# Seven block products in place of eight in ten weight units of a one-core decoder layer

## What is computed

```python
h = rms_norm(x, norm_mix)
proj = h @ w_in                      # (256, 2048) @ (2048, 832 + 3 * 1024)
c_q, c_kv, k_pe, q_sb, k_sb, v_sb = jnp.split(proj, IN_SPLITS, axis=-1)
# latent attention from c_q, c_kv, k_pe; stick-breaking attention from q_sb, k_sb, v_sb
x = x + concat(rms_norm(o_mla), rms_norm(o_sb)) @ w_out
x = x + memory_cross_attention(rms_norm(x), rms_norm(mem), ...)
x = x + hierarchical_moe(rms_norm(x), ...)      # 32 experts, 2 per token
return rms_norm(x, norm_final)
```

## Time and profile before

| | us |
|---|---|
| median of 3 runs | 1351.78 (1351.17 to 1353.06) |
| profiled execution, whole | 1350.58 |
| its span, first to last instruction | 1348.8 |
| PE busy / DVE / ACT / POOL in the span | 992.5 / 576.0 / 303.9 / 40.9 |
| bytes moved by DMA | 486.40 MB, mean 361 GB/s |

### The profile page before, as it was taken

One profiled execution on the slowest core, in us unless ns is written; L12 is line 12 of the kernel. 1 busy time (PEld: TensorE's weight loads), 2 busy tenths in 40 slices (PEclk: granted clock), 3 DMA queues, 4 the chain that ended last, 5 costly groups with the idle time before them and its releaser, 6 DMA issues.

```text
span 1348.8 us, 20643 instructions
## 1 busy us (share of the span) xinstructions
PE 992.5 (74%) x8516; PEld 595.7 (44%) x8516; DVE 576.0 (43%) x1132; ACT 303.9 (23%) x537; POOL 40.9 (3%) x92
## 2 busy tenths in 40 slices
PE   8999999999999975666555666655566655566656
PEld 7888898888888522222222222212222222222222
DVE  5555567776656643233322233332223332223324
ACT  5554457774544100000000000000000000000002
POOL 1300000130000000000000000000000000000001
PEclk9999999999999997778777778787787787777878
DMA  7777764447869999999999999999999999999997
GB/s 245 262 243 250 214 176 125 152 150 276 290 235 354 359 432 429 434 431 432 430 432 434 430 430 430 434 431 430 430 435 431 431 431 431 434 431 430 430 427 307
DMA packets 78021, 486.40 MB, mean 361 GB/s; under 512 B 9944, under 2 KB 25438, under 8 KB 64799
## 3 DMA queue, kind: packets, MB, share of 16 engines
q1 hardware_dynamic: 77484, 483.46, 89.0%
q10 hardware_dynamic: 306, 2.11, 0.4%
q0 software_dynamic: 192, 0.31, 0.2%
HBM read 481.14 MB, written 4.72 MB: 360 GB/s over the span
## 4 chain that ended last, share of the span: by engine, by line
PE 50%; DMA 46%; SPq 1%; DVE 1%; issue 1%; ACT 0%; DVEq 0%; ACTq 0%
DMA gu<-in_w_up 42%; PE ps L1053 10%; PE ps L606 8%; PE ps L608 8%; PE ps L607 8%; PE ps L1108 5%; DMA down<-in_w_down 4%; PE ps L1032 2%; PE ps L1065 1%; PE ps L586 1%; PE ps L851 1%; PE ps L852 1%; PE ps L853 1%; PE ps L778 1%; SPq L471 0%
## 5 line engine op out<-in xcount | busy, mean ns | idle before, releaser
L1053 PE MATMUL ps<-gu,xe 128*32 128x256 f32 x3968 | 284.9, 450 | 305.8 <-DMA gu<-in_w_up 305.3
L2144 DVE TENSOR_TENSOR x_sum<-ps,x_sum 128x512 f32<-128x512 f32 x240 | 149.1, 684 | 508.3 <-PE ps L1065 508.3
L1053 PEld LDWEIGHTS ps<-gu,xe 128*32 128x32 f32 x3968 | 139.7, 129 | 468.9 <-DMA gu<-in_w_up 328.5
L1619 DVE TENSOR_TENSOR w_lo<-w_raw,w_hi 128x1024 fp32r<-128x1024 f32 (+1 forms) x137 | 164.6, 1207 | 117.7 <-ACT w_hi L1226 114.2
L606 PE MATMUL ps<-w_hi,a_hi 128*128 128x512 f32 (+1 forms) x468 | 183.3, 392 | 0.0
L607 PE MATMUL ps<-w_lo,a_hi 128*128 128x512 f32 (+1 forms) x468 | 179.8, 384 | 0.0
L608 PE MATMUL ps<-w_hi,a_lo 128*128 128x512 f32 (+1 forms) x460 | 176.8, 384 | 0.0
L1226 ACT ACTIVATE w_hi<-w_raw 128x1024 fp32r<-128x1024 f32 (+1 forms) x137 | 141.9, 1040 | 128.7 <-PE ps L608 98.2
L1538 ACT ACTIVATE sg<-ps 128x128 f32<-128x128 f32 x31 | 8.6, 278 | 654.3 <-PE ps L1053 654.3
L1108 PE MATMUL ps<-down,act_t 128*32 128x512 f32 x976 | 112.4, 601 | 6.1 <-DMA down<-in_w_down 6.1
L607 PEld LDWEIGHTS ps<-w_lo,a_hi 128*128 128x128 f32 x468 | 88.0, 188 | 16.4
(11 more groups left out here) (335 smaller groups left out, 831.6 us busy)
## 6 DMA issues: line engine op xcount, KB each, us to landing
down<-in_w_down SPq DMA_DIRECT2D x29, 4096.0 KB, 22.7
gu<-in_w_gate SPq DMA_DIRECT2D x28, 4096.0 KB, 31.7
gu<-in_w_up SPq DMA_DIRECT2D x28, 4096.0 KB, 40.9
w_raw<-in_w_in SPq DMA_DIRECT2D x56, 512.0 KB, 5.1
w_raw<-in_w_out SPq DMA_DIRECT2D x32, 512.0 KB, 4.4
gu<-in_w_up SPq DMA_DIRECT2D x18, 512.0 KB, 6.1
w_raw<-in_w_mem_kv SPq DMA_DIRECT2D x16, 512.0 KB, 3.5
down<-in_w_down SPq DMA_DIRECT2D x13, 512.0 KB, 15.2
```

The source lines that it names most:

```text
L1053: mm = pe.matmul(ps[5][j * SLOTS:(j + 1) * SLOTS, 0:2 * P].rearrange("s (m f) -> s m f", m=2), xe[:, k, :], gu[side][:, :, k, j * P:(j + 1 ...
L1619: ve.tensor_tensor(w_lo[:, u % RING, :, 0:n], w_raw[:, u % RING, :, 0:n], w_hi[:, u % RING, :, 0:n], ALU.subtract).then_inc(S("w_split"), 1)
L2144: ins = ve.tensor_tensor(x_sum[:, t, cols], ps[g][:, :], (x_res if first else x_sum)[:, t, cols], ALU.add)
```

## The change

In five chunks (SB_Q, SB_Q + 1, SB_K, SB_K + 1, SB_V) the units 1 and 5 of each chunk's eight, ten units in all, are no longer multiplied as eight blocks (two row tiles x two k tiles x two column halves of 256) but as seven, by sums and differences of blocks (the Winograd form of Strassen's scheme). Each of the seven block products is three matmuls with 256 moving columns (`triple`): three block products are issued at the unit's own place, and the four that need summed weights two units later (`SEVEN_LAG`).

- **PE** (`project_sevens`): 21 matmuls of 256 columns for such a unit, in place of 12 of 512. Each of the five chunks now uses four PSUM banks, and alternating chunks use banks 0 to 3 and 4 to 7. The transposes of c_q and c_kv move into the chunks SB_K and SB_K + 1, ahead of their unit 5. New waits on `t_rounded`, `t_split` and `seven_summed`.
- **POOL** (`sum_weights`): for each such unit one subtraction of 512 columns and two of 256, linked, as soon as the unit has landed. SP reloads the slot only after them.
- **ACT**: rounds only 768 columns of such a unit, and two units later the 1024 columns of the summed weights (`t_hi`); once, after unit 11, waits for DVE and rounds the row sums (`s_hi`, 1024 columns). Chunks are copied from `seven_sum` after `rounded` of three more units. The load of `mem_sb` moves from after KV_LAT to SB_V, behind the rounding of unit 62.
- **DVE**: once, between `split_w` of unit 11 and the angle calculation, `sum_rows` (one addition of 1024 columns, four of 256), a wait for ACT's `s_hi`, and `s_lo` (1024 columns). For each of the ten units `t_lo` (1024 columns). After each of the five chunks `sum_sevens`, nine operations of 256 columns that combine the seven products.
- **SP**: `move_quads` four units later.
- Several semaphores are merged; the waits on them ask for the same events.

```diff
-MOVE_AT = [DONE[_c] + RING + 3 for _c in QUADS]
+MOVE_AT = [DONE[_c] + RING + (3 if _c == MEM_K else 7) for _c in QUADS]
+SEVENS = [SB_Q, SB_Q + 1, SB_K, SB_K + 1, SB_V]
+SEVEN_AT, SEVEN_LAG = [1, 5], 2
...
+            def triple(dst, xh, xl, wh, wl, start=False, stop=False):
+
+                pe.matmul(dst, xh, wh, start=start, stop=False)
+                pe.matmul(dst, xh, wl, start=False, stop=False)
+                return pe.matmul(dst, xl, wh, start=False, stop=stop)
...
+                    if i in SEVEN_AT:
...
+                        triple(ps[b + 2][:, left], a11h, a11l, wh[:, 0, right], wl[:, 0, right], start=m == 0)
+                        triple(ps[b][:, right], a12h, a12l, wh[:, 1, right], wl[:, 1, right])
+                        triple(ps[b][:, left], s_hi[:, m, 3], s_lo[:, m, 3], wh[:, 1, left], wl[:, 1, left]
+                               ).then_inc(S("w_used"), 1)
...
+                    n = summed_of(u)
+                    if n is not None:
...
+                        pe.wait_ge(S("t_rounded"), n + 2)
+                        pe.wait_ge(S("t_split"), n + 3)
...
-            pe.wait_ge(S("consts"), 1)
+            pe.wait_ge(S("consts"), 3)
             for c in range(KV_LAT, Q_PE):
...
+                if c == SB_Q:
+                    pe.wait_ge(S("split_lo"), KD)
+                    pe.wait_ge(S("t_rounded"), 1)
+                    pe.wait_ge(S("t_split"), 2)
...
             rounded(DONE[Q_LAT] + RING)
+            sc.wait_ge(S("t_split"), 1)
+            sc.activation(s_hi[:, :, :, :].rearrange("p m s q -> p (m s q)"),
+                          s_raw[:, :, :, :].rearrange("p m s q -> p (m s q)"), ACT.Copy).then_inc(
+                              S("t_rounded"), 1)
             sc.wait_ge(S("rstd"), 1)
...
+                    if c == SB_V:
+                        sc.wait_ge(S("t_used"), SEVEN_PAIRS)
+                        sc.dma_start(mem_sb[:, :, :], mem[0].rearrange("(t p) d -> p t d", p=P)).then_inc(
+                            S("mem_loaded"), 16)
...
+            def sum_rows():
...
+                link(ve.tensor_tensor(s_sum[:, :, :, :].rearrange("p i j q -> p i (j q)"), even[0], even[1],
+                                      ALU.add))
+                link(ve.tensor_tensor(s_raw[:, :, 0], rows(1, 0), rows(1, 1), ALU.add))
+                ve.tensor_tensor(s_raw[:, :, 2], rows(0, 0), rows(1, 0), ALU.subtract)
+                link(ve.tensor_tensor(s_raw[:, :, 1], s_raw[:, :, 0], rows(0, 0), ALU.subtract))
+                ve.tensor_tensor(s_raw[:, :, 3], rows(0, 1), s_raw[:, :, 1], ALU.subtract).then_inc(
+                    S("t_split"), 1)
...
+            sum_rows()
+            ve.wait_ge(S("t_rounded"), 1)
+            ve.tensor_tensor(s_lo[:, :, :, :].rearrange("p m s q -> p (m s q)"),
...
             from math import pi
...
             for c in range(Q_LAT, Q_PE):
...
                 split_w(DONE[c] + RING)
...
+                if c in SEVENS:
+                    sum_sevens(c)
+                    split_w(DONE[c] + RING + 3)
```

More of the change, by code:

```diff
@@ L355, in acc_bank, with seven_of, summed_of, plain_cols @@
                 return 2
+            if c in SEVENS:
+                return 0 if c % 2 else 4
             return 2 * ((c - W_OUT) % 2) if c >= W_OUT else 2 * (c % 2)
+        def seven_of(u):
+            c, i = UNITS[u]
+            return PAIRS * SEVENS.index(c) + SEVEN_AT.index(i) if c in SEVENS and i in SEVEN_AT else None
+        def summed_of(u):
+            c, i = UNITS[u]
+            return seven_of(u - SEVEN_LAG) if c in SEVENS and i >= SEVEN_LAG else None
+        def plain_cols(tile, u):
+            return tile[:, u % RING].rearrange("p k n -> p (k n)")[:, HN:UK * UN]
         def bank_user(c):
@@ L1621, in split_w @@
                                          S("w_split"), 1)
+                    m = summed_of(u)
+                    if m is not None:
+                        ve.wait_ge(S("t_rounded"), m + 2)
+                        ve.tensor_tensor(t_lo[:, m % 2, :], t_raw[:, m % 2, :], t_hi[:, m % 2, :],
+                                         ALU.subtract).then_inc(S("t_split"), 1)
                 done[0] = max(done[0], upto)
@@ new lines, in sum_sevens @@
+            def sum_sevens(c):
+                n, b = SEVENS.index(c), acc_bank(c)
+                left, right = slice(0, HN), slice(HN, UN)
+                part = [seven_part[:, g, :] for g in range(3)]
+                p1, p5, p6, p7 = (ps[b + 2 + g][:, half] for g in range(2) for half in (left, right))
+                ve.wait_ge(S("t_used"), PAIRS * (n + 1))
+                if n >= 1:
+                    ve.wait_ge(*chunk_out(SEVENS[n - 1]))
+                link(ve.tensor_copy(part[0], p1))
+                ve.tensor_tensor(part[1], p6, part[0], ALU.add)
+                link(ve.tensor_tensor(seven_sum[:, 0, right], ps[b][:, right], part[0], ALU.add))
+                ve.tensor_tensor(part[0], p5, part[1], ALU.add)
+                link(ve.tensor_tensor(part[2], p7, part[1], ALU.add))
+                ve.tensor_tensor(seven_sum[:, 0, left], ps[b][:, left], part[0], ALU.add)
+                ve.tensor_tensor(seven_sum[:, 1, right], ps[b + 1][:, right], part[2], ALU.add)
+                link(ve.tensor_tensor(part[1], p5, part[2], ALU.add))
+                ve.tensor_tensor(seven_sum[:, 1, left], ps[b + 1][:, left], part[1], ALU.add).then_inc(
+                    S("seven_summed"), 1)
```

177 lines of the change are left out of this document (142 added, 35 removed).

## The result

| | before | after |
|---|---|---|
| median of the runs of the comparison, us | 1351.74 (1350.40 to 1354.24, 9 runs) | 1356.53 (1354.15 to 1359.29, 9 runs) |
| profiled execution, whole, us | 1350.58 | 1356.74 |
| its span, us | 1348.8 | 1355.0 |
| POOL busy, us | 40.9 | 85.6 |

The changed kernel takes 1.0034 of the time before, 95% interval 1.0024 to 1.0045: 4.8 us slower by the medians. The forecast was 1352.1 us, with a range up to 1355.5, and the time lies outside it.

What follows compares the result with a forecast made beforehand. The prediction took PE to bound the first stage, with savings passing to the end. Its terms, -3.40 us saved and +3.73 us stall, summed to +0.3 us: 1352.1 us, range 1348.4 to 1355.5.

Steps and rivals of the forecast that it cites:

- What bounds the kernel: First stage: PE is the bound, and each microsecond saved on it passes to the end at full value.
- The stall at unit 12: Front: the block ahead of the angles on DVE delays unit 12's split, so PE stalls 3.7 us, bounds 2.9 to 4.7.
- Could the stall lower PE's clock? ... I take no cost: PE's clock behind the stall: granted clock stays at 1.00, as at 440 to 460 us, so no cost.
- The saving: PE in the ten units: 21 narrow matmuls at 113.3 ns save 0.340 us each, 3.40 us in all; lower end 2.1.
- The sum: Whole kernel: -3.40 us saved and +3.73 us stall give +0.3 us, 1352.1 us on the median.
- Rival A: Whole kernel: the saving and the stall at unit 12 cancel, +0.3 us, bounds -0.5 to +2.6; chance 0.60.
- Rival B: Front: no stall, the row sums are hidden and the saving arrives, 1348.4 us; chance 0.13.
- Rival C: Ahead of unit 64: mem_sb lands late, PE stands 4.1 us, 1356.2 us; chance 0.17.
- Rival D: Chunk boundaries: sum_sevens or the spill makes a unit late at four or five, 0.5 to 1 us each; chance 0.10.
- at nothing, with little to spare: SP's spill at chunk boundaries: weight loads blocked 8.3 us still arrive 2.6 us or more before need, no cost.
- The expert stage of another length: Expert stage: a length other than before was named as a sign that the forecast is wrong.

Runs made afterwards that it cites:

- e9: The kernel before with the product of high x and low w left out in all ten units: 1342.64 us, ratio 0.9939.
- e7: The kernel before with two linked 1024-column additions on DVE ahead of the angles: 1353.56 us, one time.
- e11: The kernel before with three linked 1024-column additions on DVE ahead of the angles: 1353.75 us, one time.
- e2: The kernel before with four linked 1024-column additions on DVE ahead of the angles: 1356.79 us, ratio 1.0043.
- e6: The changed kernel with 14 filler matmuls on PE in the gap ahead of unit 12: 1355.44 us, ratio 1.0029.
- e4: The kernel before with the ten units as 24 matmuls of 256 columns in place of 12 of 512: 1353.26 us, ratio 1.0016.
- e1: The changed kernel with s_hi and s_lo moved behind unit 15 and the angles behind the split of unit 23: 1350.81 us, ratio 0.9998.
- e5: As e1, but with the angles on DVE behind the split of unit 26 instead of unit 23: 1351.92 us, ratio 0.9996.
- e10: e5 with the memory tokens loaded in two 1 MB halves behind the first two copies of the query projections: 1350.68 us, ratio 0.9999.
- e15: e10 with the product of high x and low w also left out in two plain units of the first query projection: 1351.46 us, ratio 0.9998.
- e14: e10 with its PE saving taken back by 15 more narrow matmuls, added work kept: 1351.63 us, ratio 1.0003.

## Why the prediction was wrong, step by step

**What bounds the kernel**: right. Taking 9.07 us of PE work away gave 8.6 +- 0.4 us (e9), so PE sets the first stage and the later one keeps it.

**The stall at unit 12**: right in place, cause and size: 3.67 us against 3.73. The block took from 35.48 to 40.8 us, the splits began at 43.45, and the first matmul stood at 44.41.

**"Could the stall lower PE's clock? ... I take no cost"**: this is the step that failed, and it was worth 2.79 us. The evidence I used was a stretch of 20 us in which PE was idle for 2.6 us in pieces with the clock at 1.00; the longest of these pieces is 1.3 us. The stall is one piece of 3.5 us. The runs show the difference: a single piece of 0.79 us cost nothing behind it (e7), 2.04 us cost 1.62 (e11), 3.31 us cost 2.63 (e2), and with PE kept at work through the same delay the cost was gone (e6: 7.11 us for the 48 matmuls against 9.82). With this term the forecast's own sum would have been 1355, inside its range, and with the saving at 2.00 us as well 1356.3, against 1356.5 measured.

**The saving**: the mechanism was right, the term was mis-sized. I took 113.3 ns for a narrow matmul, the value that is half of 226.7, over the row that showed 117.7; it measured 118 to 119 in the new units and 120 in e4. The saving was 2.00 us, and 2.1 had been my lower end, from the line through two widths. What I gave as the reason for preferring 113.3, that the slow group stood in a slow stretch, did not carry over: e4 has the price with no work added anywhere. The Trainium skill's fixed part per matmul (TensorE: Matmul & The Clock Gate, section Back-to-back issue gap) had spoken for a loss by narrowness, and I had set it aside by the rows of 113.2; the measured 118 to 120 ns against 226.7, taken as a straight line in the columns, give such a part of 9 to 13 ns, larger than the page's; the 113.2 of rows 6 gives none.

**The sum** was -3.40 + 3.73 = +0.3; measured it is -2.00 + 3.67 + 2.79 = +4.46 to the scores, and 1350.58 + 4.46 = 1355.0 us on the profiled execution of before. The profiled after is at 1356.74; the remaining 1.7 us are 2.3 us more from the scores to the end, 1.7 of them in one group at the lowered clock (5.38 us at 483.54, where before had 3.69), less 0.6 us by which unit 8 started earlier. These last two need no cause in the change: unit 8 starts between 33.14 and 34.28 us in the 17 profiles, and the length behind the scores scatters as said below. By the medians the loss is 4.8 us.

**Rival A**, the cancelling, needed the clock to cost nothing, which is the failed step. **Rival B**, no stall, was wrong by reading, and e1, e5 and e10 show that it would also have been wrong in size: without the stall the kernel is at 0.9996 to 0.9999. **Rival C**, mem_sb late: not so in the changed kernel, 8.5 us from issue to landing against the 12.4 that it had; only in e5 and e6, with the front repaired or filled, did PE stand idle at unit 64, for 0.42 and 1.22 us. **Rival D**: no gap in the profiled after at the boundaries or behind them; in e1, e6 and e15 there are four, of 0.4 to 1.3 us, with different causes (the angles beside POOL, loads behind the spill, DVE's sums). The cover that I had called "at nothing, with little to spare" is there in some profiles and gone in others. One reading in it was wrong: I had SP's reload wait for DVE's split anyway, which comes later than POOL's sums. In after SP waited for POOL's sums ahead of six of the ten reloads, 16.5 us in total and up to 3.9, and in e10 23.6 us, up to 6.3. In these two profiles no gap on PE came of it.

**The expert stage of another length** was named as something that would prove me wrong. It differed by single groups at the lower clock: from the first scores to the end 1133.5 us before, 1135.8 after. But the profile of before is the shortest of all: the nine kernels without the new form take 1133.5 to 1136.5 us there, mean 1134.9, the eight with it 1134.3 to 1137.6, mean 1135.6. A single pair of profiles cannot show a difference of 2.3 us there.

**What stays open** is why the repaired form gains nothing measurable. e10 is 1.95 us shorter to the scores in its profile, and its runs gained 0.2 +- 0.55 us; pure cuts of 1.81, 4.53 and 9.07 us passed on. Late units (in e1, e6 and e15, 0.4 to 1.3 us each) can be a part of it. They are not needed for it: the profiled execution of e10 has none, and at 1351.03 us it is no faster than the mean of its runs, 1351.04. In it the 1.95 us were lost again behind the scores, from which it took 1136.2 us to the end, 1.3 more than the mean of the kernels without the new form. The groups at the lowered clock in the expert stage are a candidate for that; but the pure cuts met the same stage and kept their gain, and e14 leans to no cost of the added work. Only one execution of each kernel was profiled, so no cause is shown. No version here beats the kernel before by more than its runs can tell.

## What to carry to other kernels

A stall on TensorE can be priced twice: its own length, and the work behind it at half the clock. Here a single idle piece of 3.3 or 3.5 us cost another 2.6 or 2.8 us, pieces of 2.0 to 3.1 us did so in some executions and not in others, and one of 0.8 us did not. Busy shares over long stretches do not tell this; look for the longest single idle piece, and if the stall cannot be moved, give PE something to do in it.

Before a block of work goes into an in-order queue, ask who waits for the next instruction on that queue. Here moving three steps a few units back removed all 4.8 us, and it is the first thing to try when fewer products make a kernel slower. And a scheme that saves an eighth of the products by halving the matmul's width pays a part of it back per instruction: take the spacing of the narrow form from its slowest row.

## What the runs showed of the hardware that I had not expected

- The step down of the clock came with a gap as short as 2.0 us (e11): 1.62 us lost behind it, with 0.66 granted from 44 to 48 us, and nothing behind one of 0.8 us (e7). It does not come each time: behind 2.59 us of idleness the clock was 1.00 before, behind 2.42 us 0.59 in after.
- In the projections a matmul of 256 columns with a new weight each stands 118 to 120 ns behind the last, one of 512 columns 226.7 ns, though the same width also stood at 113.2 ns from 190 us on the earlier trace rows; the order of destinations makes no difference (133.76 and 133.75 us).
- A filler product of two 128 x 128 f32 tiles is two matmul records, and 28 of them took 3.29 us, 0.12 us each; the clock stayed at 1.00 through them (e6).
- A DVE operation of 64 columns grew from 0.19 to 1.23 us beside a POOL operation of 1.29 us (e1), and the whole angle calculation from 2.8 to 6.0 us. Work on POOL is not free cover for work on DVE.
- The same 32 matmuls of an expert take 3.69 or 5.38 us, by the granted clock at which they fall.
